# Recurrence levels as four 32-column products with compact merges, and the head norm's mean from one all-ones product

## What is computed

```
def hgrn2_chunk(S, q, k, v, logf):
    G = jnp.cumsum(logf, axis=1)
    decay = jnp.exp(jnp.where(causal, G[:, :, None] - G[:, None, :], -jnp.inf))
    A = jnp.einsum('bthk,bshk,btshk->bhts', q, k, decay)
    o = jnp.einsum('bhts,bshv->bthv', A, v) + jnp.einsum('bthk,bhkv->bthv', q * jnp.exp(G), S)
    ...
o = rmsnorm(o, gn_g).reshape(Bsz, T, C_WIDTH) * jax.nn.silu(gx)
```

## Time and profile before

| what | value |
|---|---|
| median of 3 runs | 3308.49 us (3307.04 to 3311.26) |
| the profiled execution's own time | 3303.76 us |
| its span (first to last instruction) | 3302.0 us |
| PE busy, share of the span | 3081.4 us, 93% |
| DVE busy | 1459.8 us, 44% |
| ACT busy | 726.5 us, 22% |
| chain that ended last, share on PE | 87% |

### The profile page before, as it was taken

The page is one execution under the profiler, slowest core; times in us unless marked ns, Lnnn a source line. Parts: engine busy times, 40 slices in busy tenths (PEclk is TensorE's granted clock), DMA queues, the critical chain, the costliest instruction groups (busy, mean ns, idle before and its releaser), DMA issues.

```text
span 3302.0 us, 45486 instructions
## 1 busy us (share of the span) xinstructions
PE 3081.4 (93%) x18140; PEld 2963.6 (90%) x18140; DVE 1459.8 (44%) x2480; ACT 726.5 (22%) x1160; POOL 97.0 (3%) x88
## 2 busy tenths in 40 slices
PE   6997699979999999999899999996979999999997
PEld 5996366879999999999799999995979999999996
DVE  6887534242333333334454545545253333333335
ACT  3111556222111111111311112111031111111111
POOL 3000000010000000000100000000010000000001
PEclk9999769989999999999999999996989999999998
DMA  3112500201111111111211111110201111111111
GB/s 122 45 45 60 209 1 1 96 19 52 52 39 45 39 39 43 40 44 34 83 40 40 40 40 40 41 39 10 113 26 45 40 44 39 45 40 44 46 38 58
DMA packets 47750, 163.13 MB, mean 49 GB/s; under 512 B 8416, under 2 KB 15888, under 8 KB 44768
## 3 DMA queue, kind: packets, MB, share of 16 engines
q1 hardware_dynamic: 42992, 148.45, 13.1%
q10 hardware_dynamic: 3456, 8.91, 0.8%
q0 software_dynamic: 1136, 3.27, 0.5%
HBM read 143.28 MB, written 18.92 MB: 49 GB/s over the span
## 4 chain that ended last, share of the span: by engine, by line
PE 87%; DVE 6%; issue 3%; ACT 3%; POOL 1%; DMA 1%; DVEq 0%; ACTq 0%; POOLq 0%; SPq 0%
PE PS L493 19%; PE PS L495 19%; PE PS L494 19%; PE PS L735 5%; PE PS L737 5%; PE PS L736 5%; PE PS L1376 4%; PE PS L1112 2%; PE PS L1141 2%; DVE HF L604 1%; PE PS L1121 1%; POOL SQ L405 1%; DVE HBL L614 1%; PE PS L1392 1%; DVE Y L959 1%
## 5 line engine op out<-in xcount | busy, mean ns | idle before, releaser
L493 PE MATMUL PS<-HAH,WH 128*128 128x384 f32 x1872 | 648.2, 346 | 21.1 <-DVE HBL L1720 5.8
L494 PE MATMUL PS<-HAL,WH 128*128 128x384 f32 x1872 | 633.1, 338 | 0.0
L495 PE MATMUL PS<-HAH,WL 128*128 128x384 f32 x1872 | 632.2, 338 | 0.0
L493 PE MATMUL PS<-HBH,WH 128*128 128x384 f32 x1872 | 625.8, 334 | 0.0
L495 PE MATMUL PS<-HBH,WL 128*128 128x384 f32 x1872 | 625.6, 334 | 0.0
L494 PE MATMUL PS<-HBL,WH 128*128 128x384 f32 x1872 | 625.5, 334 | 0.0
L481 DVE TENSOR_TENSOR WL<-WR,WH 128x1024 fp32r<-128x1024 f32 x200 | 243.2, 1224 | 561.5 <-ACT WH L476 560.0
L493 PEld LDWEIGHTS PS<-HAH,WH 128*128 128x128 f32 x1872 | 357.6, 191 | 30.9 <-issue 22.9
L735 PE MATMUL PS<-UH,WH 128*128 128x384 f32 x1056 | 360.9, 342 | 5.2 <-issue 5.0
L494 PEld LDWEIGHTS PS<-HAL,WH 128*128 128x128 f32 x1872 | 357.7, 191 | 2.8 <-issue 2.1
L737 PE MATMUL PS<-UH,WL 128*128 128x384 f32 x1056 | 359.7, 341 | 0.0
(11 more groups left out here) (196 smaller groups left out, 2663.1 us busy)
## 6 DMA issues: line engine op xcount, KB each, us to landing
WR<-w_fi_in SPq DMA_DIRECT2D x88, 512.0 KB, 3.7
WR<-w_fo_in SPq DMA_DIRECT2D x44, 512.0 KB, 3.7
WR<-w_c_in SPq DMA_DIRECT2D x32, 512.0 KB, 4.1
WR<-w_ab_in SPq DMA_DIRECT2D x20, 512.0 KB, 3.8
CACHES<-k_cache_in SPq DMA_DIRECT2D x8, 1024.0 KB, 7.5
CACHES<-v_cache_in SPq DMA_DIRECT2D x8, 1024.0 KB, 6.1
X<-x_t_in SPq DMA_DIRECT2D x3, 1536.0 KB, 11.0
x_spill<-X SPq DMA_DIRECT2D x1, 4608.0 KB, 12.3
```

What stands on the lines that cost most here:

```text
L493: nc.tensor.matmul(out, wh, hh(k, third(n)), start=(k == 0), stop=False)
L494: nc.tensor.matmul(out, wh, hl(k, third(n)), start=False, stop=False)
L495: mm = nc.tensor.matmul(out, wl, hh(k, third(n)), start=False, stop=(k == KT - 1))
```

## The change

Levels 0 to 5 need only the 32x32 blocks on the diagonal of a tile. PE now forms each tile as four products, each with 32 weight columns, 32 moving columns and all 128 contraction rows, written to partitions 0, 32, 64 and 96 of one PSUM bank, so that nine tiles fill 288 columns. Level 6 has two products of 32x32 per tile and level 7 one of 64x64: only the blocks that the level fills. Levels take the banks 3, 4, 5 in turn, so that PE waits for a merge three levels back. DVE merges a level in one instruction into the compact `AB32`; at level 5 it spreads `AB32` into `AM` by four copies, and levels 6 and 7 are plain copies into `AM`, whose other blocks are set to zero once. The compact masks are made once by DVE after step 0, and POOL builds five masks instead of seven.

In the norm ACT squares into `KD` (the last third after the sample states, which read `KD`), PE sums and spreads in one go by three all-ones products, placed at i = 10, ACT takes the root of 128x384 from PSUM into `KD` three times, DVE takes the reciprocal of `KD` in place three times, and `finish` reads `KD`.

```diff
-        def level_tiles(lv, n):
-
-            hi = NT if lv <= SLEVELS else PT_TILES
-            return range(TPT * n, min(TPT * n + TPT, hi))
+        def level_blocks(lv):
+
+            if lv <= BLEVELS:
+                return [(c * BK, c * BK, BK) for c in range(P // BK)]
+            w = 1 << (lv - 1)
+            return [(o, o + w, w) for o in range(0, P, 2 * w)]
+
+        def level_tiles(lv):
+            return NT if lv <= SLEVELS else PT_TILES
...
             def level(lv, p):
                 T.add("up")
                 need(pe, s_up, T("up"))
-                for n in range(N3):
-                    if lv == 0:
-                        need(pe, s_cn, T("hgrn") * N3)
-                    else:
-                        need(pe, s_mg, T("mg") - 2)
-                    T.add("mg")
-                    for t in level_tiles(lv, n):
-                        mm = nc.tensor.matmul(PS[:, 3 + n, tile(t % TPT)], KC[:, tile(t)], QC[:, p, tile(t)],
+                if lv == 0:
+                    need(pe, s_cn, T("hgrn") * N3)
+                if lv >= 3:
+                    need(pe, s_mg, T("mg") - 2)
+                T.add("mg")
+                for t in range(level_tiles(lv)):
+                    for k0, q0, w in level_blocks(lv):
+                        mm = nc.tensor.matmul(PS[k0:k0 + w, 3 + lv % 3, t * w:(t + 1) * w],
+                                              KC[:, t * P + k0:t * P + k0 + w], QC[:, p, t * P + q0:t * P + q0 + w],
                                               start=True, stop=True)
-                    mm.then_inc(s_lv, 1)
+                mm.then_inc(s_lv, 1)
...
             def norm_sums():
-                need(pe, s_oq, T("hgrn") * N3 + N3)
-                need(pe, s_vk, T("vk"))
-                for t in range(NT):
-                    mm = nc.tensor.matmul(PS[:, 2, TH + t:TH + t + 1], AM[:, t, :], ones[:, 0:1], start=True, stop=True)
-                mm.then_inc(s_cm, 1)
-
-            def norm_cast():
-                need(pe, s_cd, T("hgrn") + 1)
-                need(pe, s_og, T("hgrn") * N3 + N3)
                 for n in range(N3):
+                    need(pe, s_oq, T("hgrn") * N3 + n + 1)
+                    need(pe, s_og, T("hgrn") * N3 + n + 1)
                     mm = nc.tensor.matmul(PS[:, 3 + n, 0:TH], ones[:, :],
                                           KD[:, TPT * n:TPT * n + TPT, :].rearrange("p a b -> p (a b)"), start=True, stop=True)
                     mm.then_inc(s_cb, 1)
...
             def square(n):
                 need(act, s_oc, T("hgrn") * N3 + n + 1)
-                act.activation(AM[:, TPT * n:TPT * n + TPT, :], PS[:, 3 + n, 0:TH].rearrange("p (a b) -> p a b", b=P),
+                if n == N3 - 1:
+                    need(act, s_sm, T("hgrn") + 1)
+                act.activation(KD[:, TPT * n:TPT * n + TPT, :], PS[:, 3 + n, 0:TH].rearrange("p (a b) -> p a b", b=P),
                                ACT.Square).then_inc(s_oq, 1)
 
-            def root():
-                need(act, s_cm, T("hgrn") + 1)
-                act.activation(rt[:, 0:NT], PS[:, 2, TH:TH + NT], ACT.Sqrt, bias=eps[:, 0:1], scale=1.0 / P).then_inc(s_cr, 1)
+            def root(n):
+                need(act, s_cb, T("hgrn") * N3 + n + 1)
+                act.activation(KD[:, TPT * n:TPT * n + TPT, :], PS[:, 3 + n, 0:TH].rearrange("p (a b) -> p a b", b=P),
+                               ACT.Sqrt, bias=eps[:, 0:1], scale=1.0 / P).then_inc(s_cr, 1)
...
+                nt = level_tiles(lv)
+                if lv <= BLEVELS:
+                    ps = PS[:, 3 + lv % 3, 0:nt * BK].rearrange("p (a b) -> p a b", b=BK)
                     if lv == 0:
-                        ins = dve.tensor_tensor(a, ps, ident[:, :].unsqueeze(1).to_broadcast([P, nt, P]), ALU.mult)
+                        ins = dve.tensor_tensor(AB32[:, 0:nt, :], ps, blk_ident[:, :].unsqueeze(1).to_broadcast([P, nt, BK]),
+                                                ALU.mult)
                     else:
-                        ins = dve.copy_predicated(a, lvl_mask[:, lv - 1, :].unsqueeze(1).to_broadcast([P, nt, P]), ps)
-                    ins.then_inc(s_mg, 1)
-                    T.add("mg")
+                        ins = dve.copy_predicated(AB32[:, 0:nt, :],
+                                                  blk_mask[:, lv - 1, :].unsqueeze(1).to_broadcast([P, nt, BK]), ps)
+                    if lv == BLEVELS:
+                        link(dve, T, ins)
+                        for k0, q0, w in level_blocks(lv):
+                            ins = dve.tensor_copy(AM[k0:k0 + w, :, q0:q0 + w], AB32[k0:k0 + w, :, :])
+                else:
+                    for k0, q0, w in level_blocks(lv):
+                        ins = dve.tensor_copy(AM[k0:k0 + w, 0:nt, q0:q0 + w],
+                                              PS[k0:k0 + w, 3 + lv % 3, 0:nt * w].rearrange("p (a b) -> p a b", b=w))
+                ins.then_inc(s_mg, 1)
+                T.add("mg")
...
-            def diagonal():
-                need(dve, s_cr, T("hgrn") + 1)
-                link(dve, T, dve.reciprocal(ri[:, 0:NT], rt[:, 0:NT]))
-                dve.tensor_tensor(KD[:, :, :], ident[:, :].unsqueeze(1).to_broadcast([P, NT, P]),
-                                  ri[:, 0:NT].unsqueeze(2).to_broadcast([P, NT, P]), ALU.mult).then_inc(s_cd, 1)
+            def roots():
+                for n in range(N3):
+                    need(dve, s_cr, T("hgrn") * N3 + n + 1)
+                    r = KD[:, TPT * n:TPT * n + TPT, :]
+                    dve.reciprocal(r, r).then_inc(s_cd, 1)
...
+            dve.wait_ge(s_const, N_CONST)
+            dve.memset(AM[:, :, :], 0.0).then_inc(s_blk, 1)
+            for c in range(P // BK):
+                g = slice(c * BK, (c + 1) * BK)
+                dve.tensor_copy(blk_mask[g, :, :], lvl_mask[g, :, g]).then_inc(s_blk, 1)
+                dve.tensor_copy(blk_ident[g, :], ident[g, g]).then_inc(s_blk, 1)
```

More of the change, by code:

```diff
@@ L40 @@
 SLEVELS = 4
+BK = 32
+BLEVELS = 5
 SMALL = dict(cw=(0, AB * CW), cb=(124, AB), lg=(128, AB), lb=(132, AB), gain=(136, 5 * KT),
@@ L100, in encoder @@
         ones = sb("ones", [P, P])
-        lvl_mask = sb("lvl_mask", [P, LEVELS, P], U8)
+        lvl_mask = sb("lvl_mask", [P, BLEVELS, P], U8)
+        blk_mask = sb("blk_mask", [P, BLEVELS, BK], U8)
+        blk_ident = sb("blk_ident", [P, BK])
         low = sb("low", [P, 6, CH])
@@ L150, in encoder @@
             AM = s2("AM", [P, NT, P])
+            AB32 = s2("AB32", [P, NT, BK])
             TA = s2("TA", [P, TOK // 2])
@@ L256, in encoder @@
         s_og = sem("s_og")
-        s_cm = sem("s_cm")
+        s_blk = sem("s_blk")
         s_cr = sem("s_cr")
@@ L380, in sync_program @@
             sp.wait_ge(s_hgs, 16 * CH)
-        N_CONST = 4 + 5 * LEVELS
+        N_CONST = 4 + 5 * BLEVELS
         X_AB = N3 * KT
@@ L433, in pool_program @@
             n = 4
-            for lv in range(LEVELS):
+            for lv in range(BLEVELS):
                 w = 1 << lv
@@ L1359, in vturn @@
                 T.add("vk")
-                if n == 0:
-                    need(pe, s_cr, T("hgrn"))
                 for tt in range(TPT):
@@ L1382, in kturn @@
                 need(pe, s_up, T("up") + 1)
-                need(pe, s_mg, T("mg") - 2 + n)
+                need(pe, s_mg, T("mg") - 1 + (n > 0))
                 for tt in range(TPT):
@@ L1471, in c_pe @@
             with pe.Fori(0, CH // 2 - 1) as i:
-                T.enter(i, w0=2, w1=4, w2=2, up=2 * (LEVELS + 2), mg=2 * N3 * (LEVELS + 1), kt=2 * N3, vk=2 * N3, head=2, hgrn=2, sf=2)
+                T.enter(i, w0=2, w1=4, w2=2, up=2 * (LEVELS + 2), mg=2 * (LEVELS + 1), kt=2 * N3, vk=2 * N3, head=2, hgrn=2, sf=2)
                 step(0, 1)
@@ L1491, in take @@
                     if n == 0:
-                        need(act, s_mg, (T("head") - 1) * N3 * (LEVELS + 1))
+                        need(act, s_mg, (T("head") - 1) * (LEVELS + 1))
                     act.activation(FG[:, p, third(n)], src, ACT.Sigmoid).then_inc(s_cg[k], 1)
@@ L1553, in step @@
                     if i == 10:
-                        root()
+                        for m in range(N3):
+                            root(m)
                     if i == 11:
@@ L1590, in level @@
             def level(lv, p):
-                T.add("lv", N3)
+                T.add("lv")
                 need(dve, s_lv, T("lv"))
+                if 0 < lv <= BLEVELS:
+                    need(dve, s_mg, T("mg"))
                 if lv == 0:
@@ L1659, in sample_states @@
                                              in1=state_bank(b), op0=ALU.mult, op1=ALU.add).then_inc(s_sn, 1)
-            def diagonal():
-                need(dve, s_cr, T("hgrn") + 1)
-                link(dve, T, dve.reciprocal(ri[:, 0:NT], rt[:, 0:NT]))
-                dve.tensor_tensor(KD[:, :, :], ident[:, :].unsqueeze(1).to_broadcast([P, NT, P]),
-                                  ri[:, 0:NT].unsqueeze(2).to_broadcast([P, NT, P]), ALU.mult).then_inc(s_cd, 1)
```

(16 more changed lines are left out.)

2 lines of the change are left out of this document (removed).

## The result

The changed kernel takes **3253.64 us** (median of 4 runs, 3248.14 to 3256.67) beside 3309.88 of the kernel before on the same chip: a ratio of 0.9828, 95% interval 0.981 to 0.9845. Forecast were 3249, in a range from 3220 to 3290.

A forecast was written before the change was run, and what follows sets the result against it. PE was taken to bound the kernel (87% of the chain). Savings 61.7 + 18.5 less losses 10.5, 3.6, 1.8 and 5 give 59.3 us: 3303.8 to 3244.5, plus 4.7 for the median, 3249 us; range 3220 to 3290.

The forecast's parts named there:

- levels, seven shared steps: Seven steps where projection and recurrence run together: thin products cut levels from 14.8 to 6.0 us per head, saving 61.7 us.
- norm at seven head ends: Head ends: three wide DVE reciprocals delay the next level 0, losing 1.5 us per head, 10.5 in seven.
- clock: PE's idle 3.6 us at six head ends may bring the clock down, costing 5 us in all.
- clock, head 0's projection: Projection ahead of head 0's recurrence: the forecast had no clock loss there, 0 us.
- levels, last step: Last step, without a projection: eight levels at half the clock take 25.5 us instead of 44.0, saving 18.5.
- the last norm: Norm after the last head: it ends at 2301.3 instead of 2297.68, 3.6 us lost.
- masks and clearing, once: Ahead of head 0's start: nine DVE instructions, about 3 us, of which 1.2 is slack, so 1.8 lost.
- I take 0.058: PE price in us of one tile's thin products in a level, read from a run of eight 16-column records.
- 0.2 per level: Each level changes the PE array's tiling twice, at 0.1 us each time.
- 27 ns a record whatever its group: Rival on thin products in levels: a tile costs 0.22 us, kernel 15 us slower, 3324 us; chance 0.07.
- The head's end: Between heads: three 2.6 us reciprocals, level 0 at 14.0 us instead of 12.53, PE idle 3.6 us before it.

The follow-up runs named there:

- the levels alone: Changed kernel with its levels kept and the norm of before put back: 3242.15 us, ratio to before 0.9779; a head at a full clock takes 73.59 us.
- deferred run: Changed kernel with a head's norm reciprocals and finish moved behind levels 1, 2 and 4 of the next step: 3228.02 us, ratio to before 0.9739.

## Why the prediction was right, and by how much each step was off

By the traces of before, of the changed kernel and of the levels alone (73.59), in us (minus is saved):

| step | predicted | measured | from |
|---|---|---|---|
| levels, seven shared steps | -61.7 | -52.9 | 7 x (81.15 - 73.59) |
| norm at seven head ends | +10.5 | +10.4 | 7 x (75.07 - 73.59) |
| clock | +5 | +8.8 | seven heads less seven at a full clock: 14.0, before 5.2 |
| clock, head 0's projection | 0 | +1.3 | up to the g thirds 36.85 for 35.59, granted 0.92 for 0.96 |
| levels, last step | -18.5 | -20.4 | 23.5 for 44.0 |
| the last norm | +3.6 | +2.9 | rest of that step, 35.3 for 32.4 |
| masks and clearing, once | +1.8 | +1.6 | g thirds to first level 0: 14.20 for 12.57 |
| sum | -59.3 | -48.3 | the stage's rows: -48.5 |

That the median came within 5 us of the forecast is in part luck: by the traces the sum is 11 us too large, and the two profiled executions stand on opposite sides of their medians.

**Levels: the mechanism was right, the price too low.** This is the term that was mis-sized most, by 8.8 us. "I take 0.058" per tile came from one run of eight records: the first group's spacing, 0.029 us a pass, taken for the weight load's. In runs of 72 it is 0.033 to 0.036 (four records at 8.3 to 8.9 ns), so a tile's eight records are 0.066. That 32 moving columns "need no more" than 16 was right (0.76 beside 0.73). And "0.2 per level" for two changes of the tiling is 0.30. So 0.90 instead of 0.72, and 7.56 us saved per head instead of 8.8. The *27 ns a record whatever its group* rival was the right price for one group: group by group the products do cost that.

Two statements of the Trainium skill can be held against the runs. The Trainium skill (TensorE: Matmul & The Clock Gate, on why 56 ns and not 53.3) says that start-to-start never drops below about 25 ns however few the columns; here that holds inside one column group (27.7 ns) and not across four (8.3 to 8.9 ns). The Trainium skill (VectorE: DVE Perf Modes, on why the pipe has eight slices) gives the divide a repeat count of 8, from which I estimated 3.4 us; the 24 reciprocals took 2.49 to 2.56 us.

**The head's end: right.** Counted from the second g third, level 0 starts at 13.8 (1891.56 less 1877.76), forecast 14.0; reciprocals 2.5, forecast 2.6; PE's wait ahead of level 0 at most head ends 3.3, forecast 3.6. Two runs show the cause: with the short reciprocal in the levels-only run, which keeps the finish in that queue, and with the reciprocals and the finish moved out in the deferred run, the wait is gone.

**The clock: sign right, size not, and the cause only in part.** I expected half-clock stretches behind the idle head ends. They stand behind three of the six (at 1736, 1815 and 1893 us). Others stand behind the thin products of the sample states, in five heads where before had three; for those the forecast had no increase. One of each in the changed kernel:

```profile
1892.90:1896.10 3.20, 3.20 (x13) 3.20 (x12) 1.29 (x2) 0.00 (x0) 0.00 (x0) 0.53 0.65 206
1873.00:1876.00 3.00, 3.00 (x11) 3.00 (x11) 2.75 (x10) 0.00 (x0) 0.00 (x0) 0.50 0.00 0
```

The levels-only run lost as much without the long idle time (534.7 us for seven heads, 19.5 over 7 x 73.59, of which the two waits are 4.7). Its second head has no more idle time than one of the deferred kernel, about 1 us, and was granted 0.98 where that had 1.00. So idle time alone doesn't decide it, and what does stays open.

**The last step** gained 2 us more than forecast: its first levels come every 2.7 to 2.8 us, not 3.2, as 72 records take 1.19 at half the clock where I had 1.4.

**The masks: right.** The nine clearing and mask instructions take 2.6 us in a row, and PE waits 1.5 us for the k behind them, so the slack that I counted was there:

```profile
1658.66 0.73 PE L1384 MATMUL PS<-QC,KC 128*32 128x32 f32 x62 [1.47 <-DVE KC L1589]
```

The first level 0 came 2.9 us later than before all the same; the other 1.3 stand in the projection ahead of it, which is the same in both kernels and ran at half the clock for longer.

## What to carry to other kernels

Thin products in separate column groups paid here only when neighbours in the program stood in different groups, so put the loop over groups inside; then count the records that each group gets, not their moving columns (16 or 32 made no difference). A replicated result saves a spread on PE, but every later operation on it is as wide as the copy: look at what stands on that engine between it and the next thing PE needs. And once a wait at a loop's seam is uncovered, ask first whether the work ahead of it can go behind the next iteration's start; here that was worth 26 us or more, nearly half of what the change itself gave.

## What I had not expected

The forecast has no word on the order of a level's products, and exchanging two loops took back the whole 1.7%, with the same instructions. The price of a level stayed when its columns were halved (0.73 for 0.76 us), at half the clock too (1.16 for 1.19). And when the norm's wait went away, another one came to light at the loop's turn (2.6 us of PE in the levels-only run), one projection third ahead of the place where the changed kernel waits up to 3.3 us.
